# Six adaptation slabs move from TensorE bursts in the mixers to ScalarE and GpSimd in the first feed-forward; both program ends and the last gate change too

## The chip, the cores and the metric

The kernel is one program on one core of a Trainium2 chip. The metric is the device time of one execution in microseconds (us), median of the runs shown; a profiled execution gives the trace. TensorE is PE in the rows, VectorE DVE, ScalarE ACT, GpSimd POOL, and SP only issues transfers.

## What is computed

Two transformer blocks run one after the other on 256 tokens of width 1024, in float32. The first has two layers: a norm, a projection `w_in`, three kinds of attention-like mixers, an output projection, and a feed-forward of squared ReLU. The second has an "ab" and a "cd" layer, each modulated by a condition vector:

```python
for l in range(DEPTH):                       # first block, DEPTH = 2
    proj = rms_norm(x, ln1_gain[l]) @ w_in[l]
    mixed = concat(nsa_mixer(...), mla_mixer(...), retention_mixer(...))
    x = x + mixed @ w_out[l]
    h = rms_norm(x, ln2_gain[l])
    x = x + square(relu(h @ w_up[l])) @ w_down[l]
x = rms_norm(x, final_gain)

def adaln(cond, w, b):                       # second block, once per layer
    m = silu(cond) @ w + b                   # [2 conditions, 1024] @ [1024, 3072]
    return split(m, 3)                       # shift, scale, gate
# h = rms_norm(x) * (1 + scale) + shift; ...; x = x + gate * (y @ w_out)
```

The change is about `m` of the ab layer: 1024 x 3072 weights (12 MB), six slabs of 512 columns, times two conditions (`c` for the tokens, `c_ctx` for the context rows), and about the `gate` of the cd layer.

## The kernel before, in words

**Stages.** The program is a row of stages, each a block with one program per engine and semaphores between them: for each layer of the first block `project_and_prepare` (norm, `w_in`), the mixers (`small_products`, then `compress_and_retain`, then attention), `out_project`, `feed_forward`; then the stages of the ab and cd layers, and `project_and_norm`, which writes the output. Within a stage each engine executes its list strictly in order; what waits is written out by hand as `wait_ge`. A stage ends when all its engines have.

**Weights.** SP loads weights in half slabs of 1 MB into a ring of five (`load_half`; a half is loaded when the fifth before it is free, `half_used`). A large product is made of three passes on TensorE, high times high, high times low and low times high. So each part of a slab (128 x 1024 elements) is first split: ScalarE casts it to `w_hi` (`split_hi`), VectorE subtracts that from the ring into `w_lo` (`split_lo`), and TensorE multiplies (`multiply`). There are three buffers of parts, so ScalarE may cast part n only when TensorE is done with part n-3.

**First feed-forward.** `feed_forward` with layer 0 (`beside` false) runs 16 slabs, 64 parts, in the order w_up 0, w_up 1, w_down 0, w_up 2, and so on. After each w_up ScalarE takes the ReLU of four banks, VectorE squares it, ScalarE casts it to `u_hi` and VectorE subtracts into `u_lo`. GpSimd only has the norm's small powers to do.

**Adaptation.** In the kernel before each mixer stage has three slabs of the ab layer's 1024 x 3072 weights (`ada_turn`, `ada_small`, `ada_mix`). `adapt_products` multiplies one slab by the padded conditions (16 instructions in the trace), ScalarE copies the bank (`keep_adapted`), `turn_conditions` sums four partial rows per condition and turns them by products with `select`, and VectorE adds the bias (`add_biases`). These stand at three places of TensorE's list, between other small products whose inputs other engines prepare.

**Mixers.** After the small products, `compress_and_retain` has a chain that ends in the attention: TensorE's `values_of` for five retention heads, then squares (ScalarE), sums (VectorE), a power (GpSimd, line 2578), two products (VectorE, lines 2551 and 2555) and then `retained_ready`, for which TensorE waits before the first attention scores (line 1375).

**The ends.** At the start the first block has a short stage of its own: SP loads the identity, `x` and `feats`, GpSimd clears five tiles; then comes the stage with the norm. At the end `project_and_norm` multiplies the product by the gate (`mixed`, line 2917), adds it to `x` (2920), multiplies by the gain (2926), squares and sums on ScalarE, takes the root on GpSimd, scales the left half on VectorE and the right half on ScalarE (2899), and SP stores two tiles of 512 KB.

Of the kernel before, what the change touches and what calls it, by code (L numbers as in the profile page):

```python
# [10 lines left out]
ALU = mybir.AluOpType  # L11
# [3 lines left out]
P = 128  # L15
D = 1024
KC = D // P
# [47 lines left out]
LAYER_SLABS = [("w_in", W_IN_SLABS), ("ada_turn", 1), ("cmp_k", 1), ("cmp_v", 1), ("small", 1), ("ada_small", 1),  # L65
               ("ada_mix", 1), ("w_out", 2), ("ffn", 16)]


ADA_NAMES = ("ab_ada", "cd_ada")
ADA_AT = {("ada_turn", 0): (0, 0, 1), ("ada_small", 0): (0, 1, 1), ("ada_mix", 0): (0, 2, 1),  # L70
          ("ada_turn", 1): (0, 3, 1), ("ada_small", 1): (0, 4, 1), ("ada_mix", 1): (0, 5, 1),
          "cd_first": (1, 0, 2), "cd_heads": (1, 2, 2), "cd_turn": (1, 4, 1), "cd_late": (1, 5, 1)}
# [58 lines left out]
def build_program(nc, dram, out):  # L131
    plan, first, first_part = slab_plan()
    with ExitStack() as ctx:
# [45 lines left out]
        skew_here = ctx.enter_context(nc.semaphore("skew_here"))  # L179
        padded = ctx.enter_context(nc.semaphore("padded"))  # L180
# [213 lines left out]
        def norm_programs(signals, hidden, tiles, scales, shifts=None, spare=None, load_rest=None, power=None, zeros=None,  # L394
# [105 lines left out]
            def on_scalar(act, early_split=None):  # L500
                if load_rest is not None:
                    nc.scalar.copy(rstd[:, ROW_RSTD:ROW_RSTD + 1], minus_half[:, 0:1])
                    act.wait_ge(feats_here, 16)
# [24 lines left out]
            def on_tensor(pe):  # L528
                if load_rest is not None:

                    pe.wait_ge(zeros_here, 1)
                    for _ in range(5):
                        nc.tensor.matmul(banks[:, 0, 0:P], zeros, zeros, start=True, stop=True)
# [378 lines left out]
        def project_features(key, hidden, fgT, qT, kT, v_rows, silu_z, fourier_y, tables, spare, tanh_z, load_bias, mask_bias,  # L912
# [10 lines left out]
            with stage("evacuated", "bias_here", "tables_here", "gates_here", "tanh_ready", "channels_ready",  # L923
                       "gate_turned", "gate_biased", "ctx_added", "channels_copied", "tokens_ready", "tokens_copied", "product_ready",
                       "bias_masked", "fourier_gated", "fourier_high", *TURNED_SIGNALS, *CTX_ROW_SIGNALS, *CTX_SIGNALS,
# [3 lines left out]
                    bias_masked, fourier_gated, fourier_high, *signals), nc.Block() as block:  # L929
# [69 lines left out]
                def _(pool):  # L999
# [5 lines left out]
                    rows["gpsimd"](pool)  # L1005

# [764 lines left out]
        def first_block(share_hidden):  # L1771
            with ExitStack() as local:
# [89 lines left out]
                with nc.Block() as block:  # L1862
                    @block.sync
                    def _(sp):
                        sp.dma_start(ident[:], dram["ident"]).then_inc(ident_here, 16)
                        for t in range(TT):
                            sp.dma_start(x[:, t, :], dram["x"][:, t, :]).then_inc(x_tile_here[t], 16)
                        sp.dma_start(feats[:], dram["feats"]).then_inc(feats_here, 16)

                    @block.gpsimd  # L1870
                    def _(pool):
                        nc.gpsimd.memset(flat[:], 0.0).then_inc(zeros_here, 1)
# [1861 lines left out]
```

## Time and profile before

| | |
|---|---|
| median of three runs | 1077.88 us (1077.81 to 1078.22) |
| span of the profiled execution, first to last instruction | 1076.1 us |
| its own time beside the span | not recorded apart; the median is 1.8 us above the span |
| TensorE busy | 98% |
| VectorE, ScalarE, GpSimd busy | 70%, 51%, 6% |
| bytes read | 179.31 MB, 169 GB/s over the span |

The span is what the trace shows. A matmul's busy time overlaps with that of the next, so TensorE's pace is read from start times, not from durations of single instructions.

### The profile page before, as it was taken

The numbers are of one execution on the slowest core, as the hardware profiler recorded it, in microseconds if no ns is written. First come the engines' busy times: TensorE is split into PE (matmuls) and PEld (weight loads), VectorE is DVE, ScalarE is ACT, GpSimd is POOL, SyncE is SP. The second block draws the span as 40 slices with busy tenths as digits, with TensorE's granted clock in tenths as the row PEclk, the third lists the DMA queues.
The fourth block names the chain that finished last, engine by engine and source line by source line (L and its number), as shares of the span: only waits on it lengthen the run. The fifth ranks groups of instructions, "written<-read, shape, count | busy, mean of one in ns | idle before, by whom it ended". The sixth has DMA issues, their size and how long they took to land. (4 is left out here: it accounts for less than half of the span.)

```text
span 1076.1 us, 17324 instructions
## 1 busy us (share of the span) xinstructions
PE 1051.7 (98%) x6788; PEld 900.5 (84%) x6788; DVE 751.0 (70%) x1442; ACT 549.1 (51%) x993; POOL 63.4 (6%) x80
## 2 busy tenths in 40 slices
PE   8999999999999999999999999999999999999996
PEld 7877889899988886888998899888886687989865
DVE  5766757655556576777788888789898945824765
ACT  5543845544445454764444544452657833623563
POOL 1000000000000000001000000020051301000000
PEclk9999999999999999999999999999999999999998
DMA  9758056565564657325856566593326233943200
GB/s 344 263 197 344 3 157 195 162 201 191 192 196 163 196 196 266 120 84 185 185 196 196 160 199 197 189 305 133 110 93 260 78 118 107 257 140 118 60 21 40
DMA packets 55477, 183.33 MB, mean 170 GB/s; under 512 B 21092, under 2 KB 33764, under 8 KB 35940
## 3 DMA queue, kind: packets, MB, share of 16 engines
q1 hardware_dynamic: 55396, 182.22, 51.8%
q8 instruction: 54, 0.88, 0.3%
q14 instruction: 27, 0.22, 0.1%
HBM read 179.31 MB, written 2.90 MB: 169 GB/s over the span
## 5 line engine op out<-in xcount | busy, mean ns | idle before, releaser
L257 DVE TENSOR_TENSOR w_lo<-ring,w_hi 128x1024 fp32r<-128x1024 f32 x259 | 316.2, 1223 | 179.8 <-ACT w_hi L242 176.2
L242 ACT CAST w_hi<-ring 128x1024 fp32r<-128x1024 f32 x259 | 270.9, 1054 | 318.0 <-PE banks L313 317.5
L313 PE MATMUL banks<-f_hi,w_hi 128*128 128x256 f32 x512 | 144.0, 281 | 0.0
L313 PE MATMUL banks<-f_hi,w_lo 128*128 128x256 f32 x512 | 143.8, 281 | 0.0
L313 PE MATMUL banks<-f_lo,w_hi 128*128 128x256 f32 x512 | 143.8, 281 | 0.0
L313 PE MATMUL banks<-w_hi,u_hi 128*128 128x512 f32 x256 | 100.1, 391 | 0.0
L313 PE MATMUL banks<-w_hi,u_lo 128*128 128x512 f32 x256 | 99.9, 390 | 0.0
L313 PE MATMUL banks<-w_lo,u_hi 128*128 128x512 f32 x256 | 99.9, 390 | 0.0
L313 PEld LDWEIGHTS banks<-f_hi,w_hi 128*128 128x128 f32 x512 | 96.4, 188 | 0.7 <-DVE f_lo L444 0.2
L313 PEld LDWEIGHTS banks<-f_lo,w_hi 128*128 128x128 f32 x512 | 96.5, 188 | 0.5
L313 PEld LDWEIGHTS banks<-f_hi,w_lo 128*128 128x128 f32 x512 | 96.5, 188 | 0.0
L313 PE MATMUL banks<-w_hi,h_hi 128*128 128x512 f32 (+1 forms) x192 | 72.6, 378 | 0.8 <-DVE w_lo L257 0.8
L313 PE MATMUL banks<-w_hi,h_lo 128*128 128x512 f32 (+1 forms) x192 | 72.0, 375 | 0.0
L313 PE MATMUL banks<-w_lo,h_hi 128*128 128x512 f32 (+1 forms) x192 | 72.0, 375 | 0.0
L313 PE MATMUL banks<-shared_hi,w_hi 128*128 128x256 f32 (+1 forms) x192 | 62.1, 323 | 0.4 <-DVE shared_lo L469 0.4
L313 PE MATMUL banks<-shared_lo,w_hi 128*128 128x256 f32 (+1 forms) x192 | 61.2, 319 | 0.0
L313 PE MATMUL banks<-shared_hi,w_lo 128*128 128x256 f32 (+1 forms) x192 | 61.1, 318 | 0.0
L313 PEld LDWEIGHTS banks<-w_hi,u_hi 128*128 128x128 f32 x256 | 48.1, 188 | 11.0 <-DVE w_lo L257 1.2
L313 PEld LDWEIGHTS banks<-w_hi,u_lo 128*128 128x128 f32 x256 | 48.0, 188 | 10.2
L313 PEld LDWEIGHTS banks<-w_lo,u_hi 128*128 128x128 f32 x256 | 48.0, 188 | 9.5
L3218 DVE SCALAR_TENSOR_TENSOR ada_rows<-ctx_uT,ctx_w,ada_rows 128x256 f32<-128x256 f32 x120 | 52.6, 480 | 4.6 <-DVE w_lo L257 0.5
L313 PE MATMUL banks<-h_hi_cd,w_hi 128*128 128x256 f32 (+1 forms) x160 | 49.2, 307 | 0.5 <-DVE h_lo_cd L469 0.5
(421 smaller groups left out, 2167.9 us busy)
## 6 DMA issues: line engine op xcount, KB each, us to landing
ring<-in_w_up SPq DMA_DIRECT2D x32, 1024.0 KB, 5.2
ring<-in_w_down SPq DMA_DIRECT2D x32, 1024.0 KB, 5.1
ring<-in_w_in SPq DMA_DIRECT2D x23, 1024.0 KB, 5.2
ring<-in_ab_ada SPq DMA_DIRECT2D x12, 1024.0 KB, 5.9
ring<-in_cd_ada SPq DMA_DIRECT2D x12, 1024.0 KB, 5.2
ring<-in_cd_in SPq DMA_DIRECT2D x12, 1024.0 KB, 5.6
ring<-in_w_out SPq DMA_DIRECT2D x8, 1024.0 KB, 7.5
ring<-in_ab_in SPq DMA_DIRECT2D x16, 512.0 KB, 4.8
```

Of the source, the lines that this page charges most:

```text
L242: nc.scalar.copy(w_hi[:, n % PARTS, :], part_source(key, q)).then_inc(hi_ready, 1)
L257: nc.vector.tensor_tensor(w_lo[:, n % PARTS, :], part_source(key, q), w_hi[:, n % PARTS, :].bitcast(F32), ALU.subtract).then_inc(part_read ...
L313: mm = nc.tensor.matmul(dst, a, b, start=first_one and i == 0, stop=last_one and i == 2, skip_group_check=shares_bank)
L3218: ins = dve.scalar_tensor_tensor(out=to(c), in0=tap, scalar=conv_w[:, c, j:j + 1], in1=to(c), op0=ALU.mult, op1=ALU.add)
```

## The change

1. The three adaptation bursts leave each mixer stage, with their waits (`kept`, `row_kept`, `mix_kept`, `mix_turned`). Turns of heads move to other places of TensorE's list.
2. In the first feed-forward the six slabs are weighed by elementwise work. Each is loaded in four quarters (two of 1024/8 row blocks, 128 x 1024 elements, 512 KB), by transfers that GpSimd issues, into two buffers. ScalarE multiplies a quarter by condition 0 into `product`, GpSimd multiplies it in place by condition 1, then adds both products into `weighed` (two sums of 128 x 512 per slab). TensorE turns a slab with eight transposes behind each of six parts of the last two slabs, VectorE sums over the turned rows and adds the biases.
3. In the cd stage GpSimd multiplies the right two halves of the output projection's weights by the gate in the ring; `project_and_norm` then drops the gate's product for the right columns.
4. The first stage is merged into the second, nine warming products stand for five, VectorE clears the zeros for them. At the end ScalarE stores the right half of each tile, SP the left one.

```diff
+AB_ADA_SLABS, STAGED = 6, 2
+                QUARTERS = 4 * AB_ADA_SLABS
+                WEIGHED_BEHIND = [2 + 12 * j // 5 for j in range(QUARTERS)]
+                SUMMED_BEHIND = [4 * (2 * FFN_GROUPS - 2) + n + 2 for n in (0, 1, 2, 4, 5)]
+                def load_quarter(pool, j):
+                    if j >= STAGED:
+                        pool.wait_ge(quarter_done, j - STAGED + 1)
+                    pool.dma_start(staged[:, j % STAGED, :, :], dram["ab_ada"][j // 4, :, j % 4 * PART:(j % 4 + 1) * PART]
+                                   .rearrange("p (k n) -> p k n", k=2)).then_inc(ada_quarter[j % STAGED], 16)
+                def weigh_first(act, j):
+                    quarter_here(act, j)
+                    if j >= 1:
+                        act.wait_ge(first_added, j)
+                    for kk in range(2):
+                        k = 2 * (j % 4) + kk
+                        done = nc.scalar.activation(product[:, kk, :], staged[:, j % STAGED, kk, :], ACT.Copy,
+                                                    scale=cond[:, k, 0:1])
+                    done.then_inc(first_weighed, 1)
+                def weigh_second(pool, step, j):
+                    k, here = 2 * (j % 4), staged[:, j % STAGED, :, :]
+                    quarter_here(pool, j)
+                    pool.wait_ge(first_weighed, j + 1)
+                    step(nc.gpsimd.tensor_tensor(here, here, cond[:, k:k + 2, 1].unsqueeze(2).broadcast_to([P, 2, BANK]),
+                                                 ALU.mult))
+                    for v, src, done in ((0, product, first_added), (1, here, quarter_done)):
+                        to = weighed[:, j // 4, v, :]
+                        if k == 0:
+                            last = nc.gpsimd.tensor_tensor(to, src[:, 0, :], src[:, 1, :], ALU.add)
+                        else:
+                            step(nc.gpsimd.tensor_tensor(to, to, src[:, 0, :], ALU.add))
+                            last = nc.gpsimd.tensor_tensor(to, to, src[:, 1, :], ALU.add)
+                        last.then_inc(done, 1)
+                        pool.wait_ge(done, j + 1)
+                def turn_slab(pe, s):
+                    pe.wait_ge(quarter_done, 4 * (s + 1))
+                    if s >= 1:
+                        pe.wait_ge(slab_summed, s if slab_banks(s) == slab_banks(s - 1) else s - 1)
...
@@ the ScalarE list of the first feed-forward
                             split_own(split_hi, act, key, 4 * i + q)
+                            if not beside and 4 * i + q in WEIGHED_BEHIND:
+                                weigh_first(act, WEIGHED_BEHIND.index(4 * i + q))
@@ the GpSimd list of the cd stage
+                    pool.wait_ge(gates_here, 32)
+                    for half in (2, 3):
+                        i = first[next_key[key]] + half
+                        half_here(pool, i)
+                        here = ring[:, i % SLOTS, :].rearrange("p (k n) -> p k n", n=BANK)
+                        nc.gpsimd.tensor_tensor(here, here, gate_rows[:, 0, right].unsqueeze(1).broadcast_to(
+                            [P, KC // 2, BANK]), ALU.mult).then_inc(weights_gated, 1)
@@ project_and_norm
-                        nc.vector.tensor_tensor(mixed[:, t, cols], banks[:, 4 * s + t, :], gate[:, cols],
-                                                ALU.mult).then_inc(gated, 1)
+                        product = banks[:, 4 * s + t, :]
+                        if s == 0:
+                            nc.vector.tensor_tensor(mixed[:, t, cols], product, gate[:, cols], ALU.mult).then_inc(gated, 1)
```

On GpSimd's list of the first feed-forward (the names are the two staging buffers, the product and the sums), the kernel before has nothing between the norm and the next stage; now there is, for the first two of 24 quarters:

```order
L496 TENSOR_TENSOR rstd<-rstd 128x2
L2633 TENSOR_TENSOR ada_staged<-ada_staged,cond_pad 128x1024
L2638 TENSOR_TENSOR ada_weighed<-ada_product 128x512
L2638 TENSOR_TENSOR ada_weighed<-ada_staged 128x512
L2610 DMA ada_staged<-in_ab_ada 128x1024
L2633 TENSOR_TENSOR ada_staged<-ada_staged,cond_pad 128x1024
L2640 TENSOR_TENSOR ada_weighed<-ada_weighed,ada_product 128x512
L2641 TENSOR_TENSOR ada_weighed<-ada_weighed,ada_product 128x512
L2640 TENSOR_TENSOR ada_weighed<-ada_weighed,ada_staged 128x512
L2641 TENSOR_TENSOR ada_weighed<-ada_weighed,ada_staged 128x512
L2610 DMA ada_staged<-in_ab_ada 128x1024
```

So a quarter is one product of 1024 columns and two or four sums of 512.

On ScalarE's list at the start of the same stage, between the casts of the parts, before:

```order
L509 ACTIVATE f_hi<-banks,feats 128x256 x8
L436 ACTIVATE mixed,sums<-x 128x1024
L242 CAST w_hi<-ring 128x1024 x5
L2718 ACTIVATE relu<-banks 128x1024
L2720 CAST u_hi<-square 128x1024
```

and now:

```order
L435 ACTIVATE mixed,sums<-x 128x1024
L241 CAST w_hi<-ring 128x1024
L2624 ACTIVATE ada_product<-ada_staged,cond_pad 128x512 x2
L241 CAST w_hi<-ring 128x1024 x2
L2624 ACTIVATE ada_product<-ada_staged,cond_pad 128x512 x2
L241 CAST w_hi<-ring 128x1024 x2
L2624 ACTIVATE ada_product<-ada_staged,cond_pad 128x512 x2
L2786 ACTIVATE relu<-banks 128x1024
L2788 CAST u_hi<-square 128x1024
```

The two weighings of a quarter stand behind every second or third cast, and what follows them in the list waits with them.

On TensorE's list of a mixer stage, from the first turned heads (`ident,proj`) on, before:

```order
L2210 MATMUL banks<-ident,proj 128x128 x10
L326 MATMUL banks<-ring,cond_pad 32x512 x8
L386 MATMUL banks<-ring,latents 128x480 x4
L2210 MATMUL banks<-ident,proj 128x128 x8
L2236 MATMUL banks<-ring,flat 32x128 x32
L2243 MATMUL banks<-ring,latents 128x320 x4
L2210 MATMUL banks<-ident,proj 128x128 x8
L341 MATMUL banks<-select,ada_rows 128x4 x4
L2253 MATMUL banks<-select,four 128x30 x2
```

and now:

```order
L2216 MATMUL banks<-ident,proj 128x128 x18
L385 MATMUL banks<-ring,latents 128x480 x4
L2241 MATMUL banks<-ring,flat 32x128 x32
L2216 MATMUL banks<-ident,proj 128x128 x8
L2249 MATMUL banks<-select,four 128x30 x2
L2255 MATMUL banks<-ring,latents 128x320 x4
```

The first burst and its turning are gone, and eight turns of heads have moved ahead of the products with the latents.

## Rows read from the trace of the kernel before

**Rows 1.** The page: busy time of engines, and the granted clock by slices.

```profile
PE 1051.7 (98%) x6788; PEld 900.5 (84%) x6788; DVE 751.0 (70%) x1442; ACT 549.1 (51%) x993; POOL 63.4 (6%) x80
PEclk9999999999999999999999999999999999999998
```

**Rows 2.** Windows, the first feed-forward: busy us (instructions) of each engine, clock, DMA.

```profile
161.30:337.00 175.70, 175.66 (x1141) 160.51 (x1140) 100.92 (x91) 84.74 (x88) 4.14 (x5) 1.00 0.58 188
```

**Rows 3.** Waits of PE, the longest: total us, times, longest.

```profile
PE banks L533 <- PEq L1862: 3.0, 1, 3.0
```

**Rows 4.** Groups by form, VectorE, 170 to 335 us: busy, mean ns | idle before.

```profile
L257 DVE TENSOR_TENSOR w_lo<-ring,w_hi 128x1024 fp32r<-128x1024 f32 x59 | 72.2, 1225 | 64.0 <-ACT w_hi L242 62.8
L2776 DVE TENSOR_TENSOR u_lo<-square,u_hi 128x1024 fp32r<-128x1024 f32 x8 | 9.8, 1226 | 8.9 <-ACT u_hi L2720 8.9
L2774 DVE TENSOR_TENSOR square<-relu 128x1024 f32<-128x1024 f32 x8 | 9.8, 1219 | 0.0
```

**Rows 5.** Groups by form, GpSimd: the large elementwise products and sums.

```profile
L1703 POOL TENSOR_TENSOR proj_ab<-proj_ab,inverse 128x512 f32<-128x512 f32 x10 | 10.4, 1040 | 16.4 <-DVE inverse L1664 16.4
L1002 POOL TENSOR_TENSOR x<-mixed,x 128x512 f32<-128x512 f32 x2 | 2.5, 1272 | 3.6 <-POOLq L1175 3.6
L3555 POOL TENSOR_TENSOR proj_ab<-proj_ab,rstd 128x1280 f32<-128x1280 f32 x1 | 2.3, 2337 | 0.2 <-POOL rstd L3320 0.2
```

**Rows 6.** Timeline, VectorE and GpSimd at 826 us: start, duration.

```profile
826.24 0.69 DVE L3018 TENSOR_TENSOR mixed<-mixed,ada_rows 128x512 f32<-128x512 f32 x1 [1.25 <-ACT ada_rows L1737]
827.51 1.16 DVE L3018 TENSOR_TENSOR mixed<-mixed,ada_rows 128x512 f32<-128x512 f32 x1
827.08 1.04 POOL L1703 TENSOR_TENSOR proj_ab<-proj_ab,inverse 128x512 f32<-128x512 f32 x1 [1.56 <-DVE inverse L1664]
```

**Rows 7.** Timeline, VectorE and GpSimd at 167 us; GpSimd at 168 and 502 us.

```profile
167.24 2.62 DVE L257 TENSOR_TENSOR w_lo<-ring,w_hi 128x1024 fp32r<-128x1024 f32 x2
167.41 1.10 POOL L493 TENSOR_SCALAR rstd<-sums 128x2 f32<-128x2 f32 x1 [63.71 <-DVE sums L430]
168.60 0.69 POOL L494 TENSOR_TENSOR rstd<-rstd,minus_half 128x2 f32<-128x2 f32 x1
502.38 0.19 POOL L493 TENSOR_SCALAR rstd<-sums 128x2 f32<-128x2 f32 x1 [65.48 <-DVE sums L430]
```

**Rows 8.** Timeline, TensorE, transposes at the first feed-forward's start.

```profile
159.48 1.94 PE L521 MATMUL banks<-ident,x 128*128 128x128 f32 x16 [0.38 <-PEq L1175]
```

**Rows 9.** Timeline, TensorE, the first layer's mixer stage.

```profile
74.64 1.92 PE L326 MATMUL banks<-ring,cond_pad 128*32 128x512 f32 x16
76.49 3.49 PE L386 MATMUL banks<-ring,latents 128*128 128x480 f32 x8
...
85.80 0.95 PE L341 MATMUL banks<-select,ada_rows 128*128 128x4 f32 x8
86.61 0.61 PE L2253 MATMUL banks<-select,four 128*128 128x30 f32 x4
...
99.30 0.61 PE L386 MATMUL banks<-proj,mixed 128*128 128x64 f32 x4
...
105.63 0.71 PE L1375 MATMUL banks<-fT 64*128 64x128 f32 x6 [0.37 <-DVE mixed L2555]
```

**Rows 10.** SP's transfer of the gate's row; landing times of both transfers; VectorE then.

```profile
1007.49 0.32 SPq L995 DMA_DIRECT2D ada_rows<-gates  x1
...
DMA to landing us min/median/max: 4.0/8.1/12.2
...
1012.09 0.49 DVE L848 TENSOR_SCALAR x<-x,inverse 128x512 f32<-128x512 f32 x1
1014.63 1.22 DVE L257 TENSOR_TENSOR w_lo<-ring,w_hi 128x1024 fp32r<-128x1024 f32 x1
```

**Rows 11.** Timeline, the program's end: TensorE's last product, VectorE behind it.

```profile
1067.34 0.39 PE L313 MATMUL banks<-w_hi,h_hi_cd 128*128 128x512 f32 x1
1068.46 0.68 DVE L2917 TENSOR_TENSOR mixed<-banks,ada_rows 128x512 f32<-128x512 f32 x1
```

More of the change, by code:

```diff
@@ L531, in on_tensor @@
                     pe.wait_ge(zeros_here, 1)
-                    for _ in range(5):
+                    for _ in range(9):
                         nc.tensor.matmul(banks[:, 0, 0:P], zeros, zeros, start=True, stop=True)
@@ L2201, in _ @@
                 def _(sp):
-                    for i in range(first["ada_turn", layer], first["ada_mix", layer]):
+                    for i in range(first["cmp_k", layer], first["w_out", layer]):
                         load_half(sp, i + SLOTS)
@@ L2239, in _ @@
                         mm.then_inc(half_used, 1)
+                    turn_heads(2)
+                    turn_heads(3)
+                    pe.wait_ge(partial_ready, 1)
+                    for kv in range(2):
+                        mm = nc.tensor.matmul(hidden[:, kv * NC2:(kv + 1) * NC2], partial[:, kv, :], select[:, 0:NC2],
+                                              start=True, stop=True)
+                    mm.then_inc(hidden_ready, 1)
                     pe.wait_ge(act_copied, 1)
@@ L2590, in feed_forward @@
                 sb2("to_line_u", [P, 8])
+                staged, product = sb2("ada_staged", [P, STAGED, 2, BANK]), sb2("ada_product", [P, 2, BANK])
+                weighed = sb2("ada_weighed", [P, AB_ADA_SLABS, 2, BANK])
             u_hi, u_lo = (sb2(n, [P, 2, 4, SEQ], F32R) for n in ("u_hi", "u_lo"))
@@ L2632, in _ @@
                 def _(pool):
+                    if not beside:
+                        for j in range(STAGED):
+                            load_quarter(pool, j)
+                        weigh_step = InOrder(pool, weigh_steps)
                     norm["gpsimd"](pool)
                     if not beside:
+                        for j in range(QUARTERS):
+                            weigh_second(pool, weigh_step, j)
+                            if j + STAGED < QUARTERS:
+                                load_quarter(pool, j + STAGED)
                         rows["gpsimd"](pool)
@@ L2745, in _ @@
                         split_own(split_hi, act, key, 4 * i + PARTS)
+                        if not beside and 4 * i + PARTS in WEIGHED_BEHIND:
+                            weigh_first(act, WEIGHED_BEHIND.index(4 * i + PARTS))
                     split_ahead(split_hi, act, key)
@@ L2811, in _ @@
                         advance(taps, 2)
+                        if not beside and 4 * i + PARTS in SUMMED_BEHIND:
+                            sum_slab(dve, SUMMED_BEHIND.index(4 * i + PARTS))
                     advance(taps)
```

176 lines of the change are left out of this document (88 added, 88 removed).

## The prediction, made before the changed kernel ran

> **What bounds the kernel now.** I read the page first: TensorE is busy 98% of the span and its clock is granted in full in every slice but the last [rows 1]. Busy time of overlapped matmuls can mislead, so I then read TensorE's waits: the longest single one is 3.0 us, before its first product [rows 3]. So the time is TensorE's list, laid end to end. A product taken off it counts in full, unless a wait appears in its place; work given to another engine is free only while that engine delivers in time. The window of the first feed-forward shows the room: in 175.7 us TensorE works 175.66, VectorE 100.9, ScalarE 84.7, GpSimd 4.1 [rows 2]. GpSimd looks idle. The question is whether it can be used beside a VectorE that is busy 57% of the time.
>
> **What GpSimd is asked for.** One quarter is a product of 1024 columns with a broadcast factor and, in 18 of 24 quarters, four sums of 512 columns, in the other 6 two. The nearest row for the product is 2.34 us for 1280 columns, so 1.87 for 1024; for a sum of two full operands it is 1.27 us [rows 5]. That makes 24 x 1.87 + 84 x 1.27 = 44.9 + 106.7 = 151.6 us. Each of these 108 instructions waits for the one ahead of it; between two such the trace has 0.09 us (168.51 to 168.60) [rows 7], so 9.7 more: 161 us. GpSimd issues 22 transfers in between; no row shows one issued there, I take SP's 0.32 us [rows 10], 7 us (bounds 0, and 1 us each). Sum 168 us of GpSimd alone. It can start at 170 us, behind the norm's powers [rows 7].
>
> A part takes TensorE 165/59 = 2.80 us [rows 4]. ScalarE's list has the quarters behind parts 2 + 12j/5, so one per 2.4 parts, 6.7 us. GpSimd alone needs 168/24 = 7.0. That is already a little over.
>
> **What VectorE and GpSimd do to each other.** The same VectorE product of 128x512 takes 0.69 us at 826.24 and 1.16 at 827.51. In the second case GpSimd worked from 827.08 to 828.12, and VectorE ended at 828.67, 0.55 after that: it had begun, stood still until GpSimd was done, and then ran in full [rows 6]. The other way round, a GpSimd instruction on two columns takes 0.19 us at 502.38 and 1.10 at 167.41, where a subtraction of VectorE, the one that makes `w_lo`, ran from 167.24 for 1.22 us [rows 7]. So an elementwise instruction of VectorE that reads two operands from SBUF and one of GpSimd exclude each other for their whole length. In the first feed-forward all of VectorE's large instructions are of that kind: `w_lo` of each part, and two per pair of slabs for the squares, 1.22 us each [rows 4].
>
> The Trainium skill's page "SBUF — State Buffer" (Specifications, on the two sides) has this as a rule: whichever starts first holds the shared ports for the whole instruction. The rows agree, so it changes no term.
>
> Now the sum. Between parts 3 and 58 VectorE has 55 subtractions and 14 instructions of the squares: 69 x 1.22 = 84 us. Serial with GpSimd's 168 that is 252; what VectorE does inside GpSimd's own gaps (9.7 + 7 us) can be free, so 235 to 252, and I take 240. GpSimd ends at 170 + 240 = 410 us.
>
> Can it fall behind without harm? No: ScalarE has one `product` tile and waits in `weigh_first(j)` for `first_added`, in order. Behind it in its list stand the casts of the next two or three parts, and with three buffers TensorE is then out of parts. So TensorE gets 2.4 parts per quarter, one per 10 us instead of 6.7. The last quarter is weighed by ScalarE before GpSimd's last 7 us, at 403; then follow a cast and a subtraction (2.3 us), six parts (16.8) and five of the six turns. A turn is eight transposes; sixteen take 1.94 us [rows 8], so 0.95 with its start, 4.8 in all. End of the stage at 427. Before it ended at 161.3 + 64 x 2.80 = 340. **First feed-forward: +87 us** (with sums at 1.04 us, the row with a broadcast operand [rows 5], 19 less; with the product at that row's rate too, about +52; with 1 us per transfer and no free gap, +115).
>
> The page "GPSIMD Engine Reference" (2.1, Instruction dispatch) gives about 2.5 cycles per element for two inputs, an estimate of 1.07 us for 512 columns at its 1.2 GHz. The row with two full operands has 1.27, and I go by the row; with the page's figure the feed-forward would be 17 us shorter.
>
> **The mixers.** A burst takes 1.85 us (74.64 to 76.49), its turning 0.81 (85.80 to 86.61) [rows 9]. Three each: 8.0 us per layer is the most. But the attention's start waits for a chain: from the last `values_of` (99.91) to 105.63 it is 5.7 us through ScalarE, VectorE and GpSimd [rows 9], and that chain stays. Only what is removed ahead of the values counts: three bursts and one turning, 6.4 us, less the two turns of heads that now stand there (0.9) and waits that the bursts covered, about 1.1 (0.3 for `flat_ready`, 0.8 for the last copied heads). That leaves 4.4 per layer, bounds 2 and 8; TensorE then idles some 2.3 us ahead of the attention. **Two layers: -8.8.**
>
> **The cd stage.** The gate's row is issued at 1007.49 and its transfer takes 4.0 us [rows 10], so GpSimd begins at 1011.5 its two products of 2048 columns, by the 1.27 us row about 4.7 us each (3.7 by the broadcast one). VectorE's scaling at 1012.09 and its subtraction at 1014.63 [rows 10] fall into them. The scaling waits until 1016, the second product follows, and the subtraction waits for that one. VectorE would be 6.7 us late, in attention, where TensorE waits for it closely. **+5.5**, bounds 0 (if the scaling, with one operand in SBUF, doesn't count and the subtraction is covered) and 9.
>
> **The ends.** The gate's product of the last tile, 0.68 us [rows 11], and that of the tile ahead of it leave the chain: -1.4. Two stores of half size per tile, on two queues: -0.4, bounds -1 and +0.5. The merged start: the first product's 3.0 us wait [rows 3] gets shorter, but `x` has to land all the same: -0.4, bounds -1.2 and 0. Nine warming products end before `x` is there: nothing. **-2.2.**
>
> Sum: 87 - 8.8 + 5.5 - 2.2 = +81.5. On the span of 1076.1 that is 1157.6, and the median stands 1.8 above the span: **1159 us**.
>
> **The rivals.** *The engines don't exclude each other here, and GpSimd sets the pace alone.* It would end at 170 + 168 = 338, the stage at 355: +15, and the cd term falls away. 1077.9 + 15 - 11 = 1082. Against it stand both directions of [rows 6, 7]. Chance 0.06. *GpSimd keeps up* (the faster side): the quarters fit into 6.7 us, which decides at 168/24 falling under that with no exclusion, or at GpSimd instructions of half their price with it. Then the stage costs only the six turns, 5.7, and about 1 at its end, where the sums hold VectorE: 1077.9 + 6.7 - 11 = 1073.6. For it: only that rows of just this product and sum are missing. Chance 0.08. *The clock falls in the new stalls.* TensorE would idle 3 to 9 us at a time, which it never does now, so the trace can't show what its clock does. If a third of the 55 paced parts ran at half speed and nothing hid it, 18 x 2.8 = 50 us more, 1209; most would be hidden, since TensorE has 3.4 us to spare per quarter. Chance 0.08 for over 15 us. The forecast has 0.76; 0.02 is for the change to come out even by parts of the first two rivals.
>
> The Trainium skill's page "TensorE: Matmul & The Clock Gate" (Why this matters for your kernels) says that idle gaps send the engine back to the low clock; by that the third rival would be the rule, with its time as above. No row here shows it.
>
> The range 1120 to 1190 runs from the cheaper GpSimd rows (+52) to the dearer bound with a little of the clock. About 0.2% is what a measurement of this kernel can tell from no change. Faster by over that: 0.09, within it 0.03, slower 0.88.
>
> **What would show it.** In the window of the first feed-forward the stage lasts about 265 us; GpSimd is busy nearly all of it until its end, its sums show 1.3 to 2.5 us; VectorE's `w_lo` shows means above 1.22 us, up to 2; ScalarE idles at the weighing (`ada_product`) for GpSimd; TensorE waits for `w_lo`, some 80 us in all. In the mixers the attention starts 4.4 us earlier counted from the stage's start. In the cd stage one scaling of VectorE shows over 3 us. It would be wrong if GpSimd's sums take well under 1 us, if they overlap `w_lo` without either growing, or if ScalarE never waits there.

## The result, and the profile after

The changed kernel takes **1157.39 us** (median of 5 runs, 1155.76 to 1159.26); the kernel before takes 1077.88. The ratio is 1.0738, 95% interval 1.0725 to 1.0751: 7.4% slower, 1.6 us from the predicted 1159. The page's lines that answer to [rows 1]:

```profile
PE 1068.7 (92%) x6700; PEld 916.6 (79%) x6700; DVE 830.5 (72%) x1444; ACT 574.8 (50%) x1035; POOL 289.8 (25%) x214
POOL 1000039999999800000000000011012410100300
PEclk9999998888979899999999999999999999999999
```

GpSimd works from slice 6 to 14, which is the first feed-forward, and the slices in which the granted clock falls are all among these. At the ends of most stages stand a few products that TensorE makes for nobody, so their rows mark the stages. First those of the kernel before, then those of the changed one (timeline, TensorE):

```profile
72.29 0.83 PE L362 MATMUL banks<-ident 128*128 128x128 f32 x6
132.93 1.11 PE L362 MATMUL banks<-ident 128*128 128x128 f32 x8
158.26 0.83 PE L362 MATMUL banks<-ident 128*128 128x128 f32 x6
340.02 1.05 PE L362 MATMUL banks<-ident 128*128 128x128 f32 x8
405.49 0.83 PE L362 MATMUL banks<-ident 128*128 128x128 f32 x6
466.12 1.11 PE L362 MATMUL banks<-ident 128*128 128x128 f32 x8
909.25 1.60 PE L362 MATMUL banks<-ident 128*128 128x128 f32 x12
```

```profile
71.88 0.83 PE L361 MATMUL banks<-ident 128*128 128x128 f32 x6
127.96 1.11 PE L361 MATMUL banks<-ident 128*128 128x128 f32 x8
153.29 0.83 PE L361 MATMUL banks<-ident 128*128 128x128 f32 x6
418.60 1.05 PE L361 MATMUL banks<-ident 128*128 128x128 f32 x8
484.59 0.83 PE L361 MATMUL banks<-ident 128*128 128x128 f32 x6
541.56 1.11 PE L361 MATMUL banks<-ident 128*128 128x128 f32 x8
984.10 1.60 PE L361 MATMUL banks<-ident 128*128 128x128 f32 x12
```

Their differences place the whole loss:

| stretch | before | after | difference |
|---|---|---|---|
| start and first projection | 72.29 | 71.88 | -0.41 |
| mixers, layer 0 | 60.64 | 56.08 | -4.56 |
| first feed-forward | 181.76 | 265.31 | **+83.55** |
| mixers, layer 1 | 60.63 | 56.97 | -3.66 |
| 909.25 (984.10) to the end: cd stage and end | 166.85 | 172.10 | +5.25 |
| all the rest | | | -0.07 |
| span | 1076.1 | 1156.2 | +80.1 |

The stage's window (busy us and instructions of PE, PEld, DVE, ACT, POOL; clock; share of DMA; GB/s), which answers to [rows 2]:

```profile
153.29:418.60 265.31, 210.97 (x1224) 187.30 (x1222) 177.76 (x102) 115.57 (x140) 220.78 (x137) 0.88 0.53 175
```

The waits in it, first TensorE's, then ScalarE's (total us, times, longest):

```profile
PE banks L312 <- DVE w_lo L256: 48.4, 11, 8.0
PE banks L2655 <- DVE ada L2663: 5.5, 2, 3.8
```

```profile
ACT ada_product L2624 <- POOL ada_weighed L2641: 45.1, 13, 6.6
ACT ada_product L2624 <- POOL ada_weighed L2638: 12.9, 4, 5.0
ACT ada_product L2624 <- DMA ada_staged<-in_ab_ada: 9.6, 3, 7.9
```

TensorE is busy for 211 us, where a kernel below that has the same products at full clock shows 187: 24 us more because of half clock, and 54 us of waits. These two and 5.6 us of products for the six turns (187.0 against the 181.3 us that TensorE is busy in the kernel before) are the loss. GpSimd is busy 221 of 265 us.

Groups by form in this stage, GpSimd and then VectorE (170 to 400 us), which answer to [rows 4, 5]:

```profile
L2633 POOL TENSOR_TENSOR ada_staged<-ada_staged,cond_pad 128x1024 f32<-128x1024 f32 x24 | 47.0, 1959 | 0.6
L2640 POOL TENSOR_TENSOR ada_weighed<-ada_weighed,ada_product 128x512 f32<-128x512 f32 x18 | 37.1, 2059 | 1.4
...
L256 DVE TENSOR_TENSOR w_lo<-ring,w_hi 128x1024 fp32r<-128x1024 f32 x56 | 125.3, 2248 | 50.6 <-ACT w_hi L241 48.4
```

And the two engines side by side from 290 to 301 us:

```profile
290.09 0.59 POOL L2610 DMA_DIRECT2D ada_staged<-in_ab_ada  x1 [0.56 <-POOL ada_weighed L2638]
290.71 1.91 POOL L2633 TENSOR_TENSOR ada_staged<-ada_staged,cond_pad 128x1024 f32<-128x1024 f32 x1
292.69 1.29 POOL L2640 TENSOR_TENSOR ada_weighed<-ada_weighed,ada_product 128x512 f32<-128x512 f32 x1
294.07 2.16 POOL L2641 TENSOR_TENSOR ada_weighed<-ada_weighed,ada_product 128x512 f32<-128x512 f32 x1
296.30 2.16 POOL L2640 TENSOR_TENSOR ada_weighed<-ada_weighed,ada_staged 128x512 f32<-128x512 f32 x1
...
292.88 2.19 DVE L256 TENSOR_TENSOR w_lo<-ring,w_hi 128x1024 fp32r<-128x1024 f32 x1 [2.26 <-ACT w_hi L241]
295.00 2.31 DVE L2846 TENSOR_TENSOR square<-relu 128x1024 f32<-128x1024 f32 x1
298.42 1.22 DVE L2848 TENSOR_TENSOR u_lo<-square,u_hi 128x1024 fp32r<-128x1024 f32 x1 [1.12 <-ACT u_hi L2788]
```

A sum takes 1.29 us when VectorE is idle as it starts (292.69) and 2.16 when it isn't. `w_lo` takes 1.22 us alone [rows 4] and 2.19 here, the square 2.31, while `u_lo` at 298.42, which meets nobody, takes 1.22. Both grow, and they take turns: `w_lo` ends 1.09 us after the sum that was ahead of it. Alone, GpSimd would need 24 x 1.90 + 84 x 1.29 + 108 x 0.08 + 22 x 1.15 = 188 us (products, sums, the steps between them, and 0.59 us of issue with 0.56 of wait for each transfer). From the start of its first product (165.11) to the end of its last sum (399.72) it takes 234.6 and never waits for another engine for long; the 47 us between are spent behind VectorE.

That splits the loss, as an estimate: had GpSimd ended 47 us earlier and the rest of the stage stayed as it is, the stage would have lasted 219 us, 30 more than with the turns alone (188.4, below). So some 47 us are the exclusion, some 30 GpSimd's own work, which was too long for this stage in any case, and 6.6 the turns.

The cd stage, VectorE and GpSimd (answers to [rows 10]):

```profile
1085.47 4.73 DVE L848 TENSOR_SCALAR x<-x,inverse 128x512 f32<-128x512 f32 x1
1090.12 0.41 DVE L835 TENSOR_REDUCE nmax<-banks 128x1 f32<-128x256 f32 x1
...
1091.18 3.67 DVE L848 TENSOR_SCALAR x<-x,inverse 128x512 f32<-128x512 f32 x1
...
1085.36 9.20 POOL L1011 TENSOR_TENSOR ring<-ring,ada_rows 128x2048 f32<-128x2048 f32 x2 [91.06 <-DMA ada_rows<-gates]
```

Each of GpSimd's two products holds one of VectorE's scalings to its end. The last product of TensorE then starts at 1148.81 (1067.34 before, [rows 11]); with the stage's shift of 74.85 us it is 6.62 late. From there to the end it is 7.39 us instead of 8.76, so the end gains 1.37, and the two together are the +5.25 of the table.

### The profile page after: what moved, and what is told of

Read it like the earlier page. It is cut to its first block and busy times, and to the rows that moved or that the text cites. A ratio compares the mean times of both kernels' runs of the same rounds, so it can differ in the third digit from the quotient of the medians.

```text
span 1156.2 us, 17375 instructions
## 1 busy us (share of the span) xinstructions
PE 1068.7 (92%) x6700; PEld 916.6 (79%) x6700; DVE 830.5 (72%) x1444; ACT 574.8 (50%) x1035; POOL 289.8 (25%) x214
## 5 line engine op out<-in xcount | busy, mean ns | idle before, releaser
L256 DVE TENSOR_TENSOR w_lo<-ring,w_hi 128x1024 fp32r<-128x1024 f32 x259 | 372.9, 1444 | 168.1 <-ACT w_hi L241 163.4
L312 PE MATMUL banks<-f_hi,w_hi 128*128 128x256 f32 x512 | 147.7, 289 | 13.6 <-DVE w_lo L256 13.6
L312 PE MATMUL banks<-w_hi,u_hi 128*128 128x512 f32 x256 | 107.4, 420 | 34.8 <-DVE w_lo L256 34.8
L312 PEld LDWEIGHTS banks<-f_hi,w_hi 128*128 128x128 f32 x512 | 99.9, 195 | 15.4 <-DVE w_lo L256 14.1
L312 PE MATMUL banks<-w_lo,u_hi 128*128 128x512 f32 x256 | 104.9, 410 | 0.0
L312 PE MATMUL banks<-w_hi,u_lo 128*128 128x512 f32 x256 | 104.6, 409 | 0.0
L312 PEld LDWEIGHTS banks<-f_lo,w_hi 128*128 128x128 f32 x512 | 99.9, 195 | 0.6
L312 PEld LDWEIGHTS banks<-w_hi,u_hi 128*128 128x128 f32 x256 | 51.6, 202 | 48.7 <-DVE w_lo L256 38.2
L2624 ACT ACTIVATE ada_product<-ada_staged,cond_pad 128x512 f32<-128x512 f32 x48 | 32.1, 716 | 67.7 <-POOL ada_weighed L2641 45.1
L312 PEld LDWEIGHTS banks<-w_lo,u_hi 128*128 128x128 f32 x256 | 51.6, 202 | 10.0
```

The source lines that it names most:

```text
L256: nc.vector.tensor_tensor(w_lo[:, n % PARTS, :], part_source(key, q), w_hi[:, n % PARTS, :].bitcast(F32), ALU.subtract).then_inc(part_read ...
L312: mm = nc.tensor.matmul(dst, a, b, start=first_one and i == 0, stop=last_one and i == 2, skip_group_check=shares_bank)
L2624: done = nc.scalar.activation(product[:, kk, :], staged[:, j % STAGED, kk, :], ACT.Copy, scale=cond[:, k, 0:1])
```

## The experiments

All times are medians; the ratio is to the kernel before, timed in between on the same chip.

**Without the slabs.** In `feed_forward`, layer 0, loads, weighing, turns and sums are left out:

```diff
-                            weigh_second(pool, weigh_step, j)
...
-                                turn_slab(pe, 3 * (g - FFN_GROUPS + 2) + q)
...
-                                weigh_first(act, WEIGHED_BEHIND.index(4 * i + q))
...
-                                sum_slab(dve, SUMMED_BEHIND.index(4 * i + q))
```

> The changed kernel without the six slabs in the first feed-forward: no transfers, weighing, sums or turns; the adaptation of the ab layer is then its bias alone, so this part of the result is left out. Theory (the slabs' work in this stage is the whole of the stage's loss): the stage goes back from 265.3 to 181.8 us, so 1157.4 - 83.5 = 1073.9 us. Rival (the mixers without their bursts or the new start disturb the stage in another way): the stage stays above 185 us and the time above 1077 us.

Measured: 1074.61 us (1073.17 to 1081.18), ratio 0.9976 (0.9961 to 0.9992). The stage takes 181.76 us (155.74 to 337.50), as before: the slabs are the whole loss there. But ten runs spread over 8 us, where the kernel before spreads over 1, and the time goes with the clock: the mean granted clock of the execution is 0.996 in the fastest and 0.984 in the slowest. The slowest is the profiled one. The timeline ahead of the attention of layer 0 shows why, first in this kernel, then in the changed one:

```profile
101.17 2.22 PE L1383 MATMUL banks<-fT 64*128 64x128 f32 x16 [2.13 <-DVE mixed L2543]
```

```profile
100.67 1.58 PE L1383 MATMUL banks<-fT 64*128 64x128 f32 x16 [2.13 <-DVE mixed L2543]
```

The same gap of 2.13 us stands ahead of both. Behind it the clock fell in the first (0.66 from 100 to 110 us, so partly the 1.2 GHz level), not in the second. The mixers of layer 0 took 58.0 us instead of 56.1, those of layer 1 59.8 instead of 57.0. The slabs don't protect from this: the changed kernel itself shows 0.83 from 510 to 520 us, in the mixers of layer 1.

**Without the slabs, gate multiplied late.** The new `gate_half` does half 2 at the end of the cd stage's list and half 3 at the start of the last stage:

```diff
-                        nc.gpsimd.tensor_tensor(here, here, gate_rows[:, 0, right].unsqueeze(1).broadcast_to(
-                            [P, KC // 2, BANK]), ALU.mult).then_inc(weights_gated, 1)
+                    pool.wait_ge(probs_ready, n_units)
+                    gate_half(pool, next_key[key], 2, weights_gated)
...
+            for k in range(KC // 2):
+                here = ring[:, i % SLOTS, k * BANK:(k + 1) * BANK]
+                nc.gpsimd.tensor_tensor(here, here, gate_rows[:, 0, BANK:2 * BANK], ALU.mult).then_inc(done, 1)
```

> The same kernel without slabs, and the multiplication of the right weights by the gate moved: GpSimd does half 2 after VectorE's last scaling of the attention and half 3 at the start of the last stage, in pieces of 512 columns. Theory (in the cd stage the two GpSimd products of 4.6 us hold VectorE's scalings of 4.73 and 3.67 us, and nothing else is lost): the 6.6 us that the output product comes late are won back, 1073.9 - 6.6 = 1067.3 us, at most 2 us of it lost to pieces that still meet VectorE. Rival (the 6.6 us come from the gate's transfer or from the stage's other waits): no change, within 1 us of the kernel without slabs.

Measured: 1071.47 us (1067.81 to 1073.19), ratio 0.9933 (0.9914 to 0.9953). The median missed the expected 1067.3, since the same spread of the mixers lies over it; its fastest run has 1067.81. The stage marks are free of that: from the last mark to the end 165.8 us (903.98 to 1069.8), 7.5 less than without the move (906.10 to 1079.4) and 1.0 less than in the kernel before. The end alone gives 1.37, so the moved pieces cost some 0.3 us: the two large products were the loss of the cd stage. (Of the 7.5, 1.2 is that the traced execution without the move took 173.3 us here, where the changed kernel took 172.1.)

**The gap filled.** The kernel with the late gate, and products for nobody ahead of the attention:

```diff
+                keep_busy(5, 16)
                 attend_tensor(pe)
```

> The kernel without slabs and with the late gate (the adaptation of the ab layer is its bias alone), with 16 transposes of nothing that anyone reads on TensorE ahead of the attention of each mixer stage, in the place where it stood idle for 2.13 us. Theory (in that gap the granted clock falls in some executions and not in others, which spread the kernel without slabs from 1073.2 to 1081.2 us and the one with the late gate from 1067.8 to 1073.2): the fill costs nothing and holds the clock, so about 1067.5 us with a spread under 1 us. Rival (the spread comes from elsewhere, say the new start or transfers): the median stays near 1071 and the spread at several us.

Measured: 1069.78 us (1069.47 to 1069.84), ratio 0.9923 (0.9908 to 0.9938). The spread is gone in the four runs, with a clock of 0.998: the theory held on the clock. The median isn't 1067.5 since the fill was too long. A product of 128x128 with the identity is two entries in the trace, and 16 of them took 3.7 us, 1.6 more than the gap, in two layers:

```profile
98.66 3.74 PE L361 MATMUL banks<-ident 128*128 128x128 f32 x32
102.33 0.93 PE L1378 MATMUL banks<-fT 64*128 64x128 f32 x8
```

**The turns alone.** As the filled kernel, with `turn_slab` and `sum_slab` back, on zeros. GpSimd's list becomes:

```diff
-                        for j in range(QUARTERS):
-                            weigh_second(pool, weigh_step, j)
...
+                        for s in range(AB_ADA_SLABS):
+                            weigh_step(nc.gpsimd.memset(weighed[:, s, :, :], 0.0))
+                        pool.sem_inc(quarter_done, QUARTERS)
```

> The kernel with the filled gap (1069.8 us), with the six turns of eight transposes and VectorE's six sums back, but nothing loaded or weighed: the turns work on zeros, the adaptation is the bias alone. Theory (six turns at 0.95 us, 1 us at the stage's end): 1069.8 + 6.7 = 1076.5 us, 1075 to 1078. Then 10 of the 17 us of the kernel in which VectorE weighs are VectorE's lateness. Rival (the turns, whose banks must be free, are themselves the larger part): 1080 or more.

Measured: 1076.98 us (1076.76 to 1078.00). The stage takes 188.38 us, 6.6 more than 181.75; all as expected. Its row is the reference for TensorE's own work at full clock:

```profile
154.63:343.01 188.38, 186.95 (x1223) 170.24 (x1222) 110.87 (x102) 86.92 (x92) 9.81 (x11) 1.00 0.55 179
```

**GpSimd unlinked.** The kernel without slabs, with GpSimd doing ten quarters that nobody waits for:

```diff
-                    quarter_here(pool, j)
-                    pool.wait_ge(first_weighed, j + 1)
...
-                        to = weighed[:, j // 4, v, :]
+                        to = weighed[:, 0, v, :]
...
+                        for j in range(10):
+                            weigh_second(pool, weigh_step, j)
```

> The kernel without slabs, but in the first feed-forward GpSimd does the instructions of 10 quarters (a product of 1024 columns and sums of 512 each) on tiles that it has cleared itself. No other engine waits for it and it waits for none, and nothing is loaded for it; the results aren't used. Theory (VectorE and GpSimd exclude each other, but TensorE loses its time only because ScalarE waits for GpSimd): the subtractions show 1.8 to 2.3 us where they meet GpSimd, GpSimd needs 10 to 16 us per quarter where its own work is 7.4, and the stage is at most 5 us longer than without slabs: 1074 to 1079 us. Rival 1 (VectorE's delay itself starves TensorE): the stage is 20 us longer or more. Rival 2 (no exclusion, GpSimd's own instructions are just slow): the subtractions stay at 1.22 us, a quarter takes 7.4 to 8 us.

Measured: 1094.96 us (1092.01 to 1096.50), ratio 1.0160 (1.0143 to 1.0177). Nobody waits for anybody here, and still both engines are held (groups by form, GpSimd in the stage, VectorE 168 to 260 us):

```profile
L2635 POOL TENSOR_TENSOR ada_staged<-ada_staged,cond_pad 128x1024 f32<-128x1024 f32 x10 | 24.3, 2426 | 0.8
L2642 POOL TENSOR_TENSOR ada_weighed<-ada_weighed,ada_product 128x512 f32<-128x512 f32 x7 | 15.1, 2151 | 0.6
...
L256 DVE TENSOR_TENSOR w_lo<-ring,w_hi 128x1024 fp32r<-128x1024 f32 x27 | 58.0, 2164 | 16.0 <-ACT w_hi L241 15.1
```

So the exclusion is shown without any hand-over; the rival without it is out. But the theory's second half fell: at most 5 us of loss were expected, and the stage takes 200.4 us, 18.6 more:

```profile
154.00:354.38 200.38, 189.20 (x1175) 170.84 (x1174) 138.32 (x97) 86.31 (x92) 103.77 (x52) 0.96 0.52 168
```

```profile
PE banks L312 <- DVE w_lo L256: 10.7, 4, 3.7
```

VectorE's lateness alone starves TensorE: 10.7 us of waits for `w_lo`, and 7.9 us of lower clock (189.2 us busy instead of 181.3; whether the clock costs time in this kernel wasn't tested). Per 8 parts (22.4 us) VectorE has 8 subtractions and two instructions of the squares, one per 2.24 us; taking turns with GpSimd it gets one per 2.2 to 2.9 (2.92 for a square at 217.05). That is just too few. Ten quarters took 98.5 us (169.52 to 268.04), 9.85 each and so just under the expected 10 to 16, where GpSimd's own work is 66 (10 x 1.90 + 34 x 1.29 + 44 x 0.08).

**ScalarE a quarter ahead.** The changed kernel with a second tile for ScalarE's products:

```diff
-                    if j >= 1:
-                        act.wait_ge(first_added, j)
+                    if j >= 2:
+                        act.wait_ge(first_added, j - 1)
...
+                        done = nc.scalar.activation(product_of(j)[:, kk, :], staged[:, j % STAGED, kk, :], ACT.Copy,
+                                                    scale=cond[:, k, 0:1])
```

> The changed kernel with a second tile for ScalarE's products, so that ScalarE weighs a quarter ahead of GpSimd and waits only for the sums of two quarters ago. Theory (the loss is the time that VectorE and GpSimd can't use at once; with ScalarE free, GpSimd is only held more by VectorE and its last quarter comes as late): within 8 us of 1157.4. Rival (ScalarE's standing behind GpSimd is a cost of its own; a quarter took 3.5 us too long with the link and 1.9 without it): 1157.4 - 24 x 1.6 = 1119, at least 20 us less.

Measured: 1155.78 us (1153.05 to 1157.06), ratio 1.0719 (1.0704 to 1.0734): 1.6 us less in the medians, with ranges that overlap (the traced stage is 4 us shorter, but that execution was the fastest). ScalarE's waits for GpSimd's sums fell from 58 to 7 us; it stands 57 us for the quarters' data instead, whose buffers GpSimd frees no earlier:

```profile
ACT mixed L2629 <- DMA ada_staged<-in_ab_ada: 34.4, 9, 6.1
ACT ada_product L2629 <- DMA ada_staged<-in_ab_ada: 22.3, 6, 8.1
```

GpSimd is busy 91.47 us from 200 to 300 in both. So one tile more didn't free ScalarE: the other link, two staging buffers, holds it as long. What the run shows is that the pace is GpSimd's, by whichever link it reaches ScalarE. It doesn't show what ScalarE's standing costs by itself; a kernel with more staging buffers wasn't run.

**Transfers issued by SP.**

```diff
-                            if j + STAGED < QUARTERS:
-                                load_quarter(pool, j + STAGED)
...
+                            if not beside and WEIGHED_BEHIND[j - STAGED] // 2 == h:
+                                load_quarter(sp, j)
```

> The changed kernel, with the 24 transfers of slab quarters issued by SP instead of GpSimd. Theory (GpSimd's chain of work sets the pace, and each of its 22 issues costs it 0.59 us and a wait of 0.56 us ahead): 22 x 1.15 = 25 us less in the first feed-forward, 1157.4 - 25 = 1132 us; some 1125 to 1142. Rival (the pace is set by ScalarE's waits for the transfers' data or by VectorE's backlog, and the issues lie in the shade of that): within 5 us of 1157.4.

Measured: 1149.24 us (1147.21 to 1149.82), ratio 1.0655 (1.0640 to 1.0671): 8.2 us less, neither the 25 of the theory nor within the rival's 5. The stage itself is 10.5 us shorter (155.12 to 409.98), and 1.9 of that was lost again in the mixers of layer 0, where the clock fell behind the gap (0.66 from 100 to 110 us). The group of the product tells where most of the rest went:

```profile
L2633 POOL TENSOR_TENSOR ada_staged<-ada_staged,cond_pad 128x1024 f32<-128x1024 f32 x24 | 60.4, 2519 | 2.1 <-ACT ada_product L2624 0.5
```

The product behind the issue grew from 1.96 to 2.52 us, 24 x 0.56 = 13.4 us in all. The reading that fits: VectorE had used GpSimd's 1.15 us of issue and wait, and without them the product meets it. A pause of one engine is the other's working time.

**Half of the sums.**

```diff
-                            step(nc.gpsimd.tensor_tensor(to, to, src[:, 0, :], ALU.add))
-                            last = nc.gpsimd.tensor_tensor(to, to, src[:, 1, :], ALU.add)
+                            last = nc.gpsimd.tensor_tensor(to, to, src[:, 0, :], ALU.add)
```

> The changed kernel with half of each quarter's sums left out (the second row block of a quarter isn't added, so the adaptation is wrong by that part): GpSimd has a product and two sums per quarter, 4.5 us instead of 7.05. Theory (VectorE and GpSimd share one resource: per quarter 3.8 + 7.05 less 1.0 of overlap gave 9.8 us; now 3.8 + 4.5 - 1.0 = 7.3 against ScalarE's 6.7): the stage takes about 24 x 7.3 + 10 + 17 + 5 = 207 us, so 1157.4 - 58 = 1099 us, 1090 to 1107. Rival 1 (the hand-overs between ScalarE and GpSimd cost, whatever GpSimd does in between): above 1115 us. Rival 2 (it only matters whether GpSimd alone is under 6.7 us per quarter): the loss is gone but for the turns, 1081 us.

Measured: 1111.68, 1114.98 and 1122.47 us, ratio 1.0362 (1.0305 to 1.0420); a fourth execution, of 2088 us, is not in the ratio and isn't explained. The stage takes 223.8 us, where 207 were expected: the theory's range missed, and the number of rival 1, above 1115, is about met. Its window, and behind it TensorE's wait:

```profile
153.19:376.96 223.77, 196.50 (x1223) 175.09 (x1222) 168.10 (x102) 115.89 (x140) 162.40 (x101) 0.95 0.62 207
```

```profile
PE banks L312 <- DVE w_lo L256: 25.1, 12, 6.9
```

The mechanism of rival 1, the hand-overs, isn't what the trace shows: ScalarE waits for GpSimd's sums only 16 us in all, while TensorE waits 25 for `w_lo`, and half clock takes 9.5 more (196.5 to 187.0). As in the unlinked kernel it is VectorE that is late. The two engines' work added, less the overlap seen in the changed kernel, came out 17 us too low; why just 17 isn't settled.

**VectorE alone weighs.** With the late gate and the filled gap, and three staging buffers instead of two; GpSimd only issues the loads:

```diff
+                    for v in range(2):
...
+                            last = nc.vector.scalar_tensor_tensor(out=to, in0=src, scalar=cond[:, k, v:v + 1], in1=to,
+                                                                  op0=ALU.mult, op1=ALU.add)
```

> The whole computation again: late gate and filled gap, and the six slabs weighed in the first feed-forward by VectorE alone, in 96 instructions of 512 columns that multiply by the condition and add in one; GpSimd only issues the loads, ScalarE weighs nothing. By VectorE's 0.69 us for such an instruction this is 66 us on top of its 101 in a stage of 182, and nothing meets GpSimd. Theory (GpSimd's port time is the dear one, 7.05 us per quarter against 2.8 here): the stage takes 182 + 5.7 for the turns + 1 to 6 for the squares' parts, so 1067.5 + 7 to 13 = 1074 to 1080 us. Rival (VectorE at over 90% in order is late at every square): 20 us or more above 1067.5.

Measured: 1086.77 us (1086.54 to 1087.43), ratio 1.0082 (1.0067 to 1.0097), 17.0 above the filled kernel. The expected 1074 to 1080 us missed, and the rival's 20 us were nearly reached (19.3 above 1067.5). 6.6 of the stage's 16.2 us are the turns, the other 9.5 VectorE's lateness. An instruction took 0.75 us instead of 0.69; VectorE is busy 171.8 of 197.9 us:

```profile
154.77:352.68 197.91, 190.39 (x1223) 171.28 (x1222) 171.75 (x198) 86.07 (x92) 16.39 (x29) 0.99 0.69 234
```

The stage is 67 us shorter than with GpSimd's help, for the same slabs. Still this loses against the bursts: per slab the turns cost 6.6/6 = 1.1 us and VectorE's lateness 9.5/6 = 1.6, while the burst that they replace was worth 8.2/6 = 1.4.

**TensorE kept busy in the stalls.** First with 24 products of zeros in 21 places, then with 12:

```diff
+                        if not beside and p - 1 in WEIGHED_BEHIND and p > 9:
+                            for n in range(24):      # 12 in the second kernel
+                                nc.tensor.matmul(banks[:, 4, 0:P], nothing[:], nothing[:], start=False, stop=False)
```

> The changed kernel with 24 products of zeros, added to a sum that TensorE is making anyway, ahead of the part that waits for each weighing, 21 times: 58 us of work where TensorE stood still for 54 us and ran at a mean granted clock of 0.88. Theory (TensorE is paced there, so half clock costs nothing that the wait wouldn't have taken): the granted clock rises to 0.97 or more in the stage, and the time stays within 4 us of 1157.4. Rival (the lowered clock is part of the loss): 1150 us or less.

Measured: 1206.12 us (1204.14 to 1207.64). Inconclusive: a fill took 5.5 us, not 2.8, since each product is two entries in the trace as in the filled gap, and TensorE was the bound again (busy 100 of 100 us from 200 to 300).

> As the kernel with the filler, but 12 products instead of 24 in each of the 21 places. In the first try one took 0.230 us, not 0.115, so 24 of them were 5.5 us, and the stage was TensorE's again (312 us, 182 + 116 + 14). 12 are 2.76 us, 58 in all; with TensorE's own 188 at full clock 246 us, under the stage's 265. Theory (TensorE is paced, the half clock costs nothing): granted clock 0.97 or more in the stage, time within 4 us of 1157.4. Rival (the lowered clock is part of the loss): 1150 or less; or the fills stand where no wait was and add to the path: 1165 or more.

Measured: 1159.44 us (1158.34 to 1164.52), ratio 1.0766 (1.0746 to 1.0785); the changed kernel has 1157.39. Windows from 200 to 300 us, the changed kernel first, then this one:

```profile
200.00:300.00 100.00, 76.95 (x435) 67.96 (x433) 66.50 (x34) 44.91 (x55) 91.47 (x56) 0.86 0.54 179
```

```profile
200.00:300.00 100.00, 97.38 (x686) 90.66 (x686) 63.81 (x34) 46.28 (x56) 91.47 (x56) 0.98 0.54 179
```

The clock is back at 0.98, TensorE does 21 x 2.76 = 58 us of work more, and the time is the same within 2 us (the stage 266.0 us against 265.3). The half clock of the stalls was taken out of waiting time. GpSimd's busy time is the same: it has no idle time in either kernel, and its work, stretched by VectorE, sets the pace.

**The new ends on the kernel before.** Start, end and late gate, with the bursts in the mixers and no slab in the feed-forward.

> The kernel before, bursts and all, with the new start, the new end and the late gate in pieces; the whole computation. Theory (start -0.4, end -1.4, late gate at no cost): 1077.9 - 1.8 = 1076.1 us, with a spread under 1 us, since the bursts stand where the gap was. Rival (GpSimd's pieces meet VectorE in the attention's tail or the last stage): 1077 or more.

Measured: 1076.38 us (1075.85 to 1076.79), ratio 0.9985 (0.9976 to 0.9994), as expected, and with a spread of 0.9 us. It is the fastest full computation here, by 0.15%: less than the 0.2% of the prediction, though the interval leaves 1 out. All that the change's other parts gain is this; the mixers' 8 us are only to be had if the slabs cost less than that elsewhere, and neither way tried here did.

## Why the prediction was right, step by step

- **The feed-forward, +87: measured +83.55.** The mechanism is as predicted, the exclusion of VectorE and GpSimd. Products and sums were sized rightly (1.90 and 1.29 us against 1.87 and 1.27). A transfer's issue was not: 0.59 us and a wait of 0.56 ahead, against 0.32, so GpSimd's own work was 188 us and not 168. With that the serial sum is 188 + 84 = 272, not 252, and I let only 12 us overlap; GpSimd took 234.6, so some 37 us overlapped. The pauses of GpSimd are VectorE's, as the kernel with SP's issues suggests, and each meeting hides a little more. Two errors in opposite directions nearly cancelled, and that part of the good hit is luck. GpSimd also started at 165 us instead of 170.
- **The lower bound of the range.** "+52" doesn't follow from its row: at 1.04 us for 512 columns a product of 1024 would be 2.08 us, more than the 1.87 of the sum and not less. The row with a broadcast factor bears only the 19 us for the sums, so about +68, and the range should have begun near 1140.
- **How TensorE runs dry.** I put it on ScalarE, which stands in `weigh_first`. It does stand there, 58 us, and VectorE in turn waits 48 us for its `w_hi`. But it isn't the only way: with no link at all VectorE's lateness costs TensorE 1.9 us per quarter, where the linked kernel loses 3.2 (83.55 without the turns, over 24). The prediction had one carrier of two. How much of the loss goes through each in the linked kernel isn't shown, since the one looser link that was tried left ScalarE standing as long.
- **The turns, 5.7 and 1: 6.6.** These were the prediction's price should GpSimd keep up, and the kernel with the turns alone shows it.
- **The clock.** The rival had it fall at a cost; it fell (0.86 from 200 to 300 us) at none here, since TensorE was paced. "TensorE waits some 80 us" came as 54 us of waits and 24 of half clock. The Trainium skill's page "TensorE: Matmul & The Clock Gate" (Why this matters for your kernels) is borne out: behind waits of up to 8.0 us the engine did run at the low clock for part of the time. What that costs depends on whether anyone waited for TensorE.
- **The mixers, -8.8: -8.2** (4.56 and 3.66), with TensorE idle for 2.13 us ahead of the attention, against 2.3 [rows 9]. What I missed is that this gap makes the clock a gamble, worth about 2 us in layer 0 (58.0 against 56.1) and up to 3.5 in layer 1 (59.8, against 56.25 in the kernel with ScalarE a quarter ahead), with and without slabs: the kernel with SP's issues lost it in layer 0, and the changed kernel in part in layer 1.
- **The cd stage, +5.5: +6.62.** I let the second of GpSimd's products meet the subtraction; it met a second scaling (3.67 us). So nothing was hidden: the two scalings made VectorE 4.24 + 3.18 = 7.4 us late, and 6.62 of that reached the last product. That a scaling with one operand in SBUF might not count was a bound; it counts.
- **The ends, -2.2: -1.8.** Start -0.41; end -1.37, all of it the gate's products. The two queues for the stores gave nothing: from the end of the last scaling to the end of the program it is 3.67 us, and 3.62 before.

## What to carry to other kernels

Elementwise work on GpSimd isn't free because its row in the profile is empty: where VectorE reads SBUF, add the two engines' times as a first estimate of how long they take together (here 154 us of products and sums and 90 of VectorE's gave 235; with half of the sums the estimate was 17 us too low), and ask which of them does the work in less of that shared time (here VectorE alone was 67 us faster than with GpSimd's help). Before small work is taken off TensorE, ask what it covers: it may fill a gap that would cost the clock, and what replaces it may cost as much elsewhere.

## What was unexpected of the hardware

- VectorE's scaling of 128x512 with one tensor in SBUF is excluded too: 4.73 us instead of 0.49, to the end of GpSimd's product. The reduction at 1090.12, which reads PSUM alone, took its normal 0.41 us inside GpSimd's second product. The Trainium skill's page "SBUF — State Buffer" (Who interferes with whom) names `tensor_scalar` among the operations that can take the shared pair; the trace agrees, with 4.73 us here against 0.49 alone [rows 10].
- When both have work, they take turns one by one: a sum and a subtraction together take 2.2 us (the sums at 294.07 and 296.30 start 2.23 us apart), less than 1.29 + 1.22, so some 0.3 us of the two overlap.
- Behind a gap of 2.13 us on TensorE the clock fell in one traced kernel and not in another, and over ten executions of one kernel time and mean clock went together. 16 products in the gap cut a spread of 8 us (5.4 with the late gate) to 0.4.
- A transfer issued by GpSimd costs it 0.59 us and follows a wait of 0.56 us on its own last instruction; SP's row for an issue has 0.32 [rows 10].
